# A two-block transformer kernel: value tiles of the second attention moved between score steps, latent sums from f32r parts

## The reference, cut to what matters

```
proj = h @ w_in
q_lat, kv_lat, k_rope, ca_qkv = split(proj)            # 256, 128, 32, 3 * 512 columns
q  = rmsnorm(q_lat) @ w_q_up                           # 8 latent heads of 96
kv = rmsnorm(kv_lat) @ w_kv_up                         # nope keys and values
cq, ck = rmsnorm(ca q), rmsnorm(ca k); cv = ca v       # 8 heads of 64
o_ca  = softmax(cq ck^T + bias, banded by chunks of 64) cv
o_mla = softmax(q k^T) v
x = x + g * (concat(o_mla, o_ca) @ w_out)
```

## Time and profile before

| | |
|---|---|
| median of 3 runs | 1207.99 us (1207.25 to 1208.44) |
| the profiled execution | 1207.41 us, its span 1205.7 us |
| PE busy | 1177.1 us, 98% of the span |
| DVE, ACT, POOL busy | 578.6, 507.3, 452.2 us |
| DMA | 132.38 MB, mean 110 GB/s |

### The profile page before, as it was taken

One profiled execution on the slowest core, in us unless ns is written; L12 is line 12 of the kernel. 1 busy time (PEld: TensorE's weight loads), 2 busy tenths in 40 slices (PEclk: granted clock), 3 DMA queues, 4 the chain that ended last, 5 costly groups with the idle time before them and its releaser, 6 DMA issues.

```text
span 1205.7 us, 16189 instructions
## 1 busy us (share of the span) xinstructions
PE 1177.1 (98%) x5996; PEld 963.7 (80%) x5996; DVE 578.6 (48%) x1155; ACT 507.3 (42%) x791; POOL 452.2 (38%) x163
## 2 busy tenths in 40 slices
PE   6999989999999999999999999899999999999998
PEld 6887668988888888888878667678888888888887
DVE  7265355777777873312552476844633444331000
ACT  6342462633434343222454586833543334432110
POOL 5352133334443443444444300213443344434442
PEclk9999999999999999999999999999999999999999
DMA  8233122364455443223242110013222222222222
GB/s 295 88 105 105 35 71 96 118 228 174 187 209 207 176 166 102 96 96 107 88 153 105 53 36 1 36 36 105 80 95 104 104 91 83 104 72 96 96 96 94
DMA packets 27794, 132.38 MB, mean 110 GB/s; under 512 B 3296, under 2 KB 6496, under 8 KB 18784
## 3 DMA queue, kind: packets, MB, share of 16 engines
q1 hardware_dynamic: 25856, 129.25, 30.1%
q10 hardware_dynamic: 1888, 2.46, 0.7%
HBM read 129.60 MB, written 2.10 MB: 109 GB/s over the span
## 4 chain that ended last, share of the span: by engine, by line
PE 87%; issue 6%; DVE 3%; POOL 2%; ACT 1%; DMA 0%; DVEq 0%; SPq 0%; POOLq 0%
PE psum L1438 80%; PE psum L1525 2%; PE psum L1515 2%; POOL wl L460 1%; POOL wl L444 1%; DVE prob L1152 1%; PE psum L1835 1%; ACT prob L633 1%; PE psum L1923 1%; PE psum L1751 1%; DMA raw<-stream 0%; PE psum L1857 0%; DVE prob L1166 0%; PE psum L1716 0%; PE psum L1865 0%
## 5 line engine op out<-in xcount | busy, mean ns | idle before, releaser
L444 POOL TENSOR_TENSOR wl<-raw,wh 128x2048 fp32r<-128x2048 f32 (+2 forms) x94 | 389.6, 4145 | 563.9 <-ACT wh L555 293.7
L1438 PE MATMUL psum<-xh,wh 128*128 128x512 f32 (+1 forms) x1088 | 411.7, 378 | 16.4 <-POOL wl L484 9.3
L1438 PE MATMUL psum<-xl,wh 128*128 128x512 f32 (+1 forms) x1088 | 405.7, 373 | 0.0
L1438 PE MATMUL psum<-xh,wl 128*128 128x512 f32 (+1 forms) x1088 | 405.6, 373 | 0.0
L1438 PEld LDWEIGHTS psum<-xh,wh 128*128 128x128 f32 x1088 | 205.7, 189 | 59.5 <-POOL wl L484 9.3
L1438 PEld LDWEIGHTS psum<-xh,wl 128*128 128x128 f32 x1088 | 205.7, 189 | 35.9
L1438 PEld LDWEIGHTS psum<-xl,wh 128*128 128x128 f32 x1088 | 205.8, 189 | 35.1 <-issue 0.5
L1103 DVE SCALAR_TENSOR_TENSOR scratch<-psum,cols,scratch 128x511 f32<-128x511 f32 (+1 forms) x176 | 131.6, 748 | 196.3 <-ACT scratch L690 188.0
L555 ACT ACTIVATE wh<-raw 128x2048 fp32r<-128x2048 f32 (+1 forms) x52 | 91.1, 1752 | 258.2 <-PE psum L1438 258.2
L1438 PE MATMUL psum<-acth,wh 128*128 128x512 f32 (+1 forms) x374 | 141.0, 377 | 0.0
L1438 PE MATMUL psum<-acth,wl 128*128 128x512 f32 (+1 forms) x374 | 140.8, 377 | 0.0
(11 more groups left out here) (239 smaller groups left out, 1254.1 us busy)
## 6 DMA issues: line engine op xcount, KB each, us to landing
raw<-stream SPq DMA_DIRECT2D x70, 1024.0 KB, 4.7
ada_raw<-ada SPq DMA_DIRECT2D x48, 512.0 KB, 5.2
raw<-down SPq DMA_DIRECT2D x32, 704.0 KB, 4.1
raw<-stream SPq DMA_DIRECT2D x4, 512.0 KB, 4.7
outT<-h SPq DMA_DIRECT2D x8, 256.0 KB, 5.2
rel<-rel_tiles ACTq DMA_DIRECT2D x1, 1344.0 KB, 9.5
h<-xT SPq DMA_DIRECT2D x2, 512.0 KB, 5.8
h<-xT SPq DMA_DIRECT2D x1, 1024.0 KB, 10.1
```

Source lines behind the costliest of these rows:

```text
L444: pool.tensor_tensor(wl[slot][:, 0:w], raw[slot][:, 0:w], wh[slot][:, 0:w].bitcast(F32), ALU.subtract).then_inc(lo_done, 1)
L1438: ins = pe.matmul(out, lhs[a], rhs[b], start=first and n == 0, stop=last and n == 2)
```

## The change

Six things are changed.

1. Values: PE works tile by tile, both chunks of a tile in turn (`values_half`). Tiles 0 and 1 come before the second attention, tiles 2 and 3 as four half tiles beside its steps 0 to 3. Their PSUM banks are others, VectorE copies tiles 2 and 3 at its steps 2 and 4, and the split of the two chunks that follow is done in quarters at steps 4 to 11.
2. Latent sums: ScalarE rounds the three squares to f32r (`lat_high`), VectorE makes the remainders (`lat_low`), and PE sums six f32r products with a matrix `ones_all` in place of three fp32 ones.
3. The first attention's ScalarE order: the copy of the transposes now stands ahead of the exponential, as in the other two attentions, and the quarters of a chunk are done in three steps, one sooner.
4. VectorE takes the reciprocal of the row sums ahead of the step's other extra work.
5. Latent heads: the last key pair comes before query heads 4 and 5 on PE, its turn on VectorE (`key_heads(3)`) before the latent attention in place of inside its step 0.
6. GpSimd makes the low parts of the chunk `mq` in quarters.

```diff
-        P2 = {"kv": 1, "rope": 2, "ql": [3, 4], "q": [5, 7, 9, 11], "k": [6, 8, 10, 12], "v0": 13, "v": [14, 15, 16, 17]}
+        P2 = {"kv": 1, "rope": 2, "ql": [3, 4], "q": [5, 7, 9, 11], "k": [6, 8, 10, 12], "v": [13, 14, 15, 17], "v_first": 16}
-        V2_BANKS = bank[4:6] + bank[0:2]
+        V2_BANKS = bank[4:8]
...
-                    turning = TURN_LAG <= step < STEPS + TURN_LAG
-                    if before is not None:
-                        before(step)
-                    if turning and a:
+                    if TURN_LAG <= step < STEPS + TURN_LAG:
                         turned(step)
...
-                    if turning and a == 0:
-                        turned(step)
...
-                    split_quarter(7 + p, x, p1.mm, P1["k"][p])
+                    for y in ((0,), (1, 2), (3,), ())[x]:
+                        split_quarter(7 + p, y, p1.mm, P1["k"][p])
...
+            def lat_square_high(b, sq):
+                act.wait_ge(head.sq, b + 1)
+                act.activation(lat_high[b][:, :], sq[:, :], ACT.Copy).then_inc(head.hi, 1)
...
-            split_next(base + 6, p2.mm, P2["v0"])
...
-                if 2 <= step < 6:
-                    split_quarter(base + 7, step - 2, p2.mm, P2["v"][TB - 1])
+                n = step // TB - 1
+                if 0 <= n < 2:
+                    for x in ((0, 1), (2,), (), (3,))[step % TB]:
+                        split_quarter(base + 6 + n, x, p2.mm, (P2["v_first"], P2["v"][TB - 1])[n])
...
+            def lat_square_low(b, sq):
+                dve.wait_ge(head.hi, b + 1)
+                dve.tensor_tensor(lat_low[b][:, :], sq[:, :], lat_high[b][:, :].bitcast(F32), ALU.subtract).then_inc(head.lo, 1)
+
+            lat_square_low(0, sq2[0])
...
             dve.tensor_copy(k_rope[0:64, :], k_rope[64:P, :]).then_inc(rope.dve, 1)
+
+            lat_square_low(1, sq2[1])
+            lat_square_low(2, scratch[3])
...
-                if step == 0:
-                    key_heads(3)
...
-            def head_sum(job, out, ones_of, squares):
-                pe.wait_ge(head.sq, N_SQ[job])
-                for n, sq in enumerate(squares):
-                    ins = pe.matmul(out[:, :], ones_of[:, :], sq[:, :], start=n == 0, stop=n == len(squares) - 1)
+            def lat_sum(out, parts):
+                pe.wait_ge(head.lo, parts[-1] + 1)
+                for n, b in enumerate(parts):
+                    pe.matmul(out[:, :], ones_all[:, :], lat_high[b][:, :], start=n == 0, stop=False)
+                    ins = pe.matmul(out[:, :], ones_all[:, :], lat_low[b][:, :], start=False, stop=n == len(parts) - 1)
                 ins.then_inc(head.ss, 1)
...
-            n = BASE2["cv"]
-            tokens_tiles(V2_BANKS, range(TB), (n % 2, (n + 1) % 2), n, p2.mm, pairs_taken)
+            n = BASE2["cv"]
+
+            def values_half(t, c):
+
+                for kk in range(4):
+                    k = 4 * c + kk
+                    ins = split_product(V2_BANKS[t][:, :], inputs(k, P * t, P * t + P), weights((n + c) % 2, 512 * kk, 512 * kk + 512),
+                                        k == 0, k == KD - 1)
+                if c or t == TB - 1:
+                    ins.then_inc(p2.mm, 1)
+
+            pe.wait_ge(lo_done, n + 2)
+            for t in range(2):
+                pe.wait_ge(head.done, 3 + t)
+                values_half(t, 0)
+                values_half(t, 1)
+                if t == 0:
+                    pair_sums(PAIRS - 1)
...
+            def last_values_and_first_heads(step):
+                if step < 4:
+                    t, c = 2 + step // 2, step % 2
+                    if c == 0:
+                        pe.wait_ge(head.done, 2 * PAIRS - 3 + t)
+                    values_half(t, c)
```

More of the change, by code:

```diff
@@ L182, in build @@
                 sq_low = [sb(f"sq_low{b}", [P, T], F32R, s2) for b in range(2)]
+                lat_high = [sb(f"lat_high{b}", [P, T], F32R, s2) for b in range(3)]
+                lat_low = [sb(f"lat_low{b}", [P, T], F32R, s2) for b in range(3)]
+                ones_all = sb("ones_all", [P, P], F32R, s2)
             prob2 = [sb(f"prob2{b}", [P, 2, T], F32, s) for b in range(4)]
@@ L521, in _ @@
             constant(pool.memset(chunk_mask[:, :], 0.0))
+            constant(pool.tensor_copy(ones_all[:, :], ones[:, :]))
             draft = cq[:, 0, 0:P]
@@ L611, in heads_high, with attend @@
                 act.activation(head_tiles(a, p)[0], HEADS_BANKS[p % 2][:, :], ACT.Copy).then_inc(heads.hi, 1)
-            def attend(a, prob, probT, neg_max, row_sum, col0, beside=None, before=None):
+            def attend(a, prob, probT, neg_max, row_sum, col0, beside=None):
                 def turned(step):
@@ L1153, in attend @@
                                                      -1.0, FAR, ALU.add, ALU.min, neg_max[:, c + e:c + e + 1]).then_inc(att.raw if a == 2 else att.max, 1)
-                        if a == 2:
-                            dve.wait_ge(att.raw, 2 * step + 2)
-                            dve.tensor_tensor(neg_max[:, c:c + 2], neg_max[:, c:c + 2], rq[:, 2 * step:2 * step + 2], ALU.mult).then_inc(att.max, 2)
-                        if beside is not None:
-                            beside(step)
-                    if NORM_LAG <= step < STEPS + NORM_LAG:
+                    norming = NORM_LAG <= step < STEPS + NORM_LAG
+                    if norming:
                         v = step - NORM_LAG
@@ L1163, in attend @@
                         dve.reciprocal(row_sum[:, c:c + 2], row_sum[:, c:c + 2]).then_inc(att.rinv, 1)
+                    if step < STEPS:
+                        if a == 2:
+                            now = col0 + 2 * step
+                            dve.wait_ge(att.raw, 2 * step + 2)
+                            dve.tensor_tensor(neg_max[:, now:now + 2], neg_max[:, now:now + 2], rq[:, 2 * step:2 * step + 2], ALU.mult).then_inc(att.max, 2)
+                        if beside is not None:
+                            beside(step)
+                    if norming:
                         dve.wait_ge(att.rinv, V + 1)
@@ L1373, in _, with values @@
                     dve.scalar_tensor_tensor(out[:, p, :], bank[c_bank(p) + which][:, :], col(g), r[:, :], ALU.mult, ALU.mult).then_inc(head.done, 1)
-            for t in range(TB):
+            def values(t):
                 dve.wait_ge(p2.mm, P2["v"][t])
                 dve.tensor_copy(v2[:, t, :], V2_BANKS[t][:, :]).then_inc(p2.dve, 1)
-            dve.wait_ge(setup2, 11)
+            values(0)
+            values(1)
+            dve.wait_ge(setup2, 12)
             dve.wait_ge(rel_landed[0], 32)
@@ L1401, in first_heads, with last_values @@
                     query_head(step - STEPS - 1)
-            attend(1, prob2, neg_max2, row_sum2, 0, rest_of_rel, None, first_heads)
+            def last_values(step):
+                if step in (2, 4):
+                    values(1 + step // 2)
+            attend(1, prob2, neg_max2, row_sum2, 0, rest_of_rel, last_values, first_heads)
             query_head(2)
@@ L1466, in normed_pair @@
                                 ins.then_inc(mm, 1)
-            def tokens_tiles(banks, order, slots, n0, mm, ready=None):
-                for c in range(2):
-                    pe.wait_ge(lo_done, n0 + c + 1)
-                    for t in order:
-                        if c == 0 and ready is not None:
-                            ready(t)
-                        for kk in range(4):
-                            k = 4 * c + kk
-                            ins = split_product(banks[t][:, :], inputs(k, P * t, P * t + P), weights(slots[c], 512 * kk, 512 * kk + 512),
-                                                k == 0, k == KD - 1)
-                        if c == 1 or t == order[-1]:
-                            ins.then_inc(mm, 1)
             def norm_sum(norm, j, acc, count):
```

90 lines of the change are left out of this document (46 added, 44 removed).

## The result

The changed kernel takes 1221.33 us (1220.94 to 1221.63, 4 runs), against 1208.22 for the kernel before on the same chip: ratio 1.010, 95% interval 1.0081 to 1.0118, so 10 to 14 us slower. The predicted 1216.7 has the right sign and is 4.6 too low; the range ended at 1220.3.

What follows compares the result with a forecast made beforehand. PE bounds the kernel, busy 1177.1 of 1205.7 us. Terms -1.7 - 2.2 + 4.3 + 8.7 + 1.7 - 1.9 + 1.0 - 1.2 = +8.7 on 1207.41 give 1216.1, plus 0.6: 1216.7 us, range 1211.8 to 1220.3.

Steps and rivals of the forecast that it cites:

- Values, +8.7: Ahead of value tile 0: PE stops at 661.46 and waits for the second chunk's low parts until 670.15, +8.7 us.
- The clock behind it, +1.7: Behind the values' hole: PE falls to the slow clock, +1.7 us at least; a colder start could make it 2.3.
- Latent sums, +4.3: Fourth ones_all product: PE waits 3.95 us for lat_low; +2.6 us of delay and 1.7 of slow clock, +4.3.
- The -1.7: First attention, chunk quarters one step sooner: PE's 1.75 us hole at 136.10 goes, with nothing to spare, -1.7 us.
- the -2.2: First attention, copy first in steps 11 to 15: output projection starts at 169.7 in place of 171.9, -2.2 us.
- the same durations: First attention, steps 11 to 14: ScalarE's operations carried through from 156.9 with unchanged durations, last mixing copy ending 168.8.
- the old fall of the clock: Kernel before, after the hole ending 160.34: clock 0.63 and 0.52 for 3.96 us, counted as 1.7 us of PE time.
- Interleaving, -1.9 + 1.0: Second attention: value half tiles fill idle PE in steps 0 to 6, -1.9 us; moved quarters and GpSimd work cost +1.0.
- allowed 0.4: Second attention: 0.4 us allowed for four changes back from scores to f32r, taking the gain from -2.3 to -1.9.
- Latent heads, -1.2: Start of the latent attention: key_heads(3) moved ahead shortens PE's 1.65 us wait at 758.61, -1.2 us, between 0 and -2.8.
- the spread of +1.5 us: First attention: the forecast's own spread, -2.9 to +1.5 us around its value.
- 1.75 didn't: Claim from the rows that only the 1.95 us hole brought the slow clock and the 1.75 us one didn't.

Runs made afterwards that it cites:

- without the second chunk: Changed kernel with every value half tile using the first chunk's weights and waiting for that chunk alone: 1211.17 us, ratio to before 1.0005.
- the experiment with GpSimd held: Kernel before with the latent sums from f32r parts, GpSimd's subtraction waiting until all three lat_low are made: 1208.58 us, ratio 0.9989.
- the last quarter late: Kernel before with copy and reciprocal first, quarters sooner, but the last chunk's quarters one per step, the fourth in the drain: 1202.46 us, ratio 0.9953.
- part 5 alone: Kernel before with only key pair 3 ahead of query heads 4 and 5 and its VectorE turn before the latent attention: 1206.69 us, ratio 0.9984.
- the run of part 1: Kernel before with only the values' new order and the chunk quarters (ScalarE, GpSimd) that go with it: 1218.18 us, ratio 1.0063.
- the runs of parts 3 and 4 alone: Kernel before with only copy of the transposes first, quarters in three steps and one sooner, and reciprocal first: 1206.83 us, ratio 0.9985.
- the values chunk by chunk: Changed kernel with value tiles 0 and 1 taken chunk by chunk, pair 3's sums before the wait for the second chunk: 1215.15 us, ratio to before 1.0041.
- The two fastest: Kernel before with parts 3, 4, 5 and the late last quarter: 1201.15 us; the same with part 2 and GpSimd held: 1201.93 us.

## Why the prediction was right and wrong

- **Values, +8.7**: right, 8.6 by the starts. The hole is 8.43 and released by GpSimd, and without the second chunk it is gone.
- **The clock behind it, +1.7**: right in mechanism, too small. The old fall lay within 3.96 us; this one covers the last 4.3 us of the hole and the first 5.9 of the products. Between the values' first product and the sums of pair 3 PE lost 2.9 us. The step that failed is "the clock: +1.7 again, at least", which took the length of one fall for that of every fall; that is 1.2 us.
- **Latent sums, +4.3**: right, 4.4 by the trace; hole 3.84 for 3.95, and the experiment with GpSimd held shows the cause. The Trainium skill, SBUF — State Buffer, section "Who interferes with whom", says that such an operation contends with GpSimd's reads, and the runs agree: 3.17 us beside GpSimd, 0.69 without.
- **First attention, -1.7 and -2.2**: -3.9 forecast, -0.4 measured. The -1.7 was right: the first hole is gone, and PE goes from 0.2 us ahead (the start) to 1.9. The step that failed is the -2.2. The copy first did its part, and at the transposes (156.41 for 160.34) PE is 3.9 ahead. But I carried ScalarE's operations through with "the same durations" and looked at VectorE's only at the end. That took from the sooner quarters their cost: they move GpSimd's subtraction from 168.66 to 163.60, into the middle of VectorE's steps 14 and 15. At the output projection PE is 1.95 ahead, so the -2.2 is gone, and the fall of the clock behind the new 3.25 us hole takes 1.5 more. With the last quarter late, the output projection comes 4.6 us sooner. The Trainium skill's rule that I used for the sums (SBUF — State Buffer, section "Who interferes with whom") applied here as well, and I didn't ask it. Its list names `tensor_scalar` too, which the `prob` rows bear out (1.37 against 0.35). I had also counted the old fall of the clock as 1.7 us of loss; by the runs of parts 1 and 5 it cost 0.9.
- **Interleaving, -1.9 + 1.0**: -0.4 by the trace for -0.9, from pair 3's sums (666.89 and 682.38) to the second attention's last product (724.57 and 739.67). Between the same two operations (to the end of the last product) the stretches divide it (stretch, length, busy us, clock, DMA; first the kernel before, then the changed one):

```profile
666.89:725.40 58.51, 55.76 (x399) 39.18 (x397) 34.87 (x125) 38.73 (x98) 10.74 (x6) 1.00 0.13 46
```

```profile
682.38:740.50 58.12, 56.64 (x399) 38.87 (x397) 36.10 (x123) 37.42 (x99) 8.51 (x8) 1.00 0.10 37
```

PE has no idle time in the steps with values (from 682.38 to 704.00), as forecast; behind them it idles 1.48 us where it was 0.49, the forecast +1.0. But PE's busy time for the same products is 0.9 us longer, and for the changes between forms I had allowed 0.4, a term that no row had shown.
- **Latent heads, -1.2**: -1.7 by the trace, -1.5 in the trace of part 5 alone. The reciprocal first, which I had costed at nothing, is worth up to 0.4 there.

The two misses, 3.5 and 1.2 us, make up the 4.6 by which the prediction was low. That the misses at the interleaving and the heads, 0.5 us each, cancel is luck. The sign and the two large costs held with their mechanisms; at the end of the first attention the mechanism was missed, and the spread of +1.5 us that I gave it didn't hold the 3.5.

## What to carry to other kernels

When an edit moves a split or a load sooner, follow it to the end: here a quarter of 0.6 us on ScalarE moved 5.5 us of GpSimd's work, and what that collides with on VectorE decided the sign of half the gain. A loop order that needs two weight chunks at once must be set against the moment at which the second one's slot comes free, before any gain from interleaving is counted. And a slow clock costs less than its loss of products where PE also waits for others: 0.9 us in place of 1.7 in the first attention's last steps.

## What the runs showed that I had not expected

The fall of PE's clock isn't told by the length of a hole. It came behind holes of 1.65, 1.75, 1.96, 2.12, 3.25, 3.84, 5.95 and 8.43 us. But the same 1.75 and 1.65 had none in the kernel before, 1.96 had none in the run of part 1, and the hole of 3.2 us ahead of the output projection had one in the changed kernel and none in the runs of parts 3 and 4 alone and of the values chunk by chunk, which run the same operations there. It came around 692 us in two runs, with no hole over 1.1 us near. By the trace's record of the clock it lasted 3.4, 6.8 or 10.2 us, and 3.4 or 6.8 behind the same hole of 3.84. So a new hole on PE's own path costs its length, and 0 to 3 us more that one execution doesn't tell; why it falls behind some holes and not behind others stays open. The prediction's "1.75 didn't" was read from one execution.

The kernels that have such places spread by 2 to 7 us from run to run (the changed one, in four runs, by 0.7). The two fastest, in whose profiles the clock never fell in mid-program, spread by 0.3 and 1.2 (that of the late quarter alone, whose profile shows no fall either, by 2.1).
